# Gate and value projection units moved between attention's steps and the linear attention's levels, two barriers taken out, attention scores two deep

## What is computed

```
def trunk_layer(x, cond, lp, lam_init, cache):
    sh1, sc1, g1, sh2, sc2, g2, sh3, sc3, g3 = jnp.split(cond.astype(x.dtype), N_MOD, -1)
    ...
    h = x * (1.0 + sc2) + sh2
    m, new_cache = token_mixer(h, lp, lam_init, cache)
    x = layer_norm(ALPHA * x + g2 * m, lp['ln_g'][1], lp['ln_b'][1])
    ...

def token_mixer(h, lp, lam_init, cache):
    p = h @ lp['w_in']
    p_rw, p_gla, p_diff = jnp.split(p, [RW_IN, RW_IN + GLA_IN], -1)
    ...
    o_rw, s_rw = rwkv7_branch(p_rw, s_rw0, lp)
    o_gla, s_gla = gla_branch(p_gla, s_gla0, lp)
    o_diff, new_k, new_v = diff_branch(p_diff, ctx_kv, lp, lam_init)
    mixed = jnp.concatenate([o_rw, o_gla, o_diff.astype(F32)], -1)
    out = mixed @ lp['w_out']
```

## Time and profile before

| what | value |
|---|---|
| median of 3 runs | 2019.07 us (2018.96 to 2021.9) |
| the profiled execution's own time | 2014.65 us |
| its span (first to last instruction) | 2012.7 us |
| PE, DVE, ACT busy | 95%, 51%, 36% of the span |
| chain of work that ended last | PE 83%, DVE 9%, ACT 4%, waiting for nothing shown 2% |

### The profile page before, as it was taken

The page is one execution under the profiler, slowest core; times in us unless marked ns, Lnnn a source line. Parts: engine busy times, 40 slices in busy tenths (PEclk is TensorE's granted clock), DMA queues, the critical chain, the costliest instruction groups (busy, mean ns, idle before and its releaser), DMA issues.

```text
span 2012.7 us, 37360 instructions
## 1 busy us (share of the span) xinstructions
PE 1913.7 (95%) x16184; PEld 1724.1 (86%) x16184; DVE 1019.8 (51%) x1639; ACT 726.2 (36%) x1210; POOL 32.5 (2%) x66
## 2 busy tenths in 40 slices
PE   7999999998899899999999999999988789999997
PEld 5999997987679769999989999989867787899996
DVE  2333334555566775333355333366557757633335
ACT  3322224444442353222252222255364325422222
POOL 0000000000000001000000000000000000000000
PEclk9999999999989999999999999999999899999999
DMA  8733336333581145333344333323345003433330
GB/s 343 303 125 125 124 123 234 105 119 132 227 334 43 36 158 190 125 124 124 124 156 146 125 124 125 125 84 126 108 159 209 4 4 137 159 124 124 123 109 32
DMA packets 41472, 277.70 MB, mean 138 GB/s; under 512 B 4778, under 2 KB 6810, under 8 KB 9344
## 3 DMA queue, kind: packets, MB, share of 16 engines
q1 hardware_dynamic: 35424, 255.34, 35.1%
q0 software_dynamic: 3312, 16.91, 2.2%
q10 hardware_dynamic: 2608, 3.56, 0.5%
HBM read 269.22 MB, written 3.41 MB: 135 GB/s over the span
## 4 chain that ended last, share of the span: by engine, by line
PE 83%; DVE 9%; ACT 4%; issue 2%; DMA 1%; ACTq 0%; PEldq 0%; DVEq 0%; SPq 0%; PEld 0%
PE bank L923 17%; PE bank L992 17%; PE bank L927 17%; PE bank L926 17%; PE bank L760 2%; PE bank L1380 1%; PE bank L1369 1%; DMA ring<-weights 1%; PE bank L1387 1%; DVE ring_r L2193 1%; PE bank L841 1%; ACT arena L1663 1%; PE bank L769 1%; DVE arena L2203 1%; DVE arena L2229 1%
## 5 line engine op out<-in xcount | busy, mean ns | idle before, releaser
L2193 DVE TENSOR_TENSOR ring_r<-ring,arena_r 128x1024 fp32r<-128x1024 f32 x328 | 387.9, 1222 | 679.3 <-ACT arena_r L1658 678.6
L923 PE MATMUL bank<-arena_r 128*128 128x384 f32 (+3 forms) x2052 | 702.2, 342 | 8.9 <-DVE arena_r L2237 6.7
L927 PE MATMUL bank<-arena_r,ring_r 128*128 128x384 f32 (+2 forms) x1812 | 602.0, 332 | 0.0
L926 PE MATMUL bank<-arena_r 128*128 128x384 f32 (+2 forms) x1812 | 599.7, 331 | 0.0
L923 PEld LDWEIGHTS bank<-arena_r 128*128 128x128 f32 x2052 | 386.5, 188 | 31.6 <-issue 15.7
L1658 ACT ACTIVATE arena_r<-ring 128x1024 fp32r<-128x1024 f32 x340 | 340.7, 1052 | 144.4 <-PE bank L927 138.9
L926 PEld LDWEIGHTS bank<-arena_r 128*128 128x128 f32 x1812 | 340.9, 188 | 3.4
L927 PEld LDWEIGHTS bank<-arena_r,ring_r 128*128 128x128 f32 x1812 | 340.1, 188 | 0.0
L992 PE MATMUL bank<-arena_r 128*128 128x512 f32 x1128 | 310.6, 393 | 0.3 <-issue 0.3
L1812 ACT ACTIVATE arena<-bank 128x384 f32<-128x384 f32 x88 | 43.2, 491 | 738.4 <-PE bank L927 738.4
L992 PEld LDWEIGHTS bank<-arena_r 128*128 128x128 f32 x1128 | 210.8, 188 | 43.1 <-issue 1.2
(11 more groups left out here) (301 smaller groups left out, 1809.6 us busy)
## 6 DMA issues: line engine op xcount, KB each, us to landing
ring<-weights SPq DMA_DIRECT2D x242, 1024.0 KB, 4.9
lnrow<-ln_in POOLq DMA_DIRECT2D x6, 1024.0 KB, 6.5
const<-consts POOLq DMA_DIRECT2D x1, 2211.0 KB, 10.0
arena<-gate POOLq DMA_DIRECT2D x4, 385.0 KB, 7.5
x<-x_in ACTq DMA_DIRECT2D x1, 1536.0 KB, 13.7
rows<-row_in POOLq DMA_DIRECT2D x2, 704.0 KB, 10.4
par<-par_in POOLq DMA_DIRECT2D x2, 662.5 KB, 7.5
y_out<-x SPq DMA_DIRECT2D x2, 512.0 KB, 2.6
```

Of the source, the lines that this page charges most:

```text
L923: mm = pe.matmul(out, w_h, h_h, start=start, stop=False, skip_group_check=True)
L926: pe.matmul(out, w_h, h_l, start=False, stop=False, skip_group_check=True)
L927: return pe.matmul(out, w_l, h_h, start=False, stop=stop, skip_group_check=True)
L2193: ve.tensor_tensor(low_unit((l, name), u) if out is None else out, raw, place.bitcast(F32), ALU.subtract).then_inc(w_ready, 1)
```

## The change

It moves the GLA gate and value units out of `project`. The gates' 12 blocks (4 units x 3 groups, `gate_block`) stand in attention's steps, three in step 0 and one in each of steps 1 to 9; the values' three blocks (`value_block`) stand at the beginning of `gla` and before levels 1 and 2. Their rounding moves with them: units 6 to 9 in steps 1, 4, 7 and 10 on ACT and 2, 5, 8 and 11 on DVE. The gates are copied out of PSUM in ACT's step 10, and Silu is applied later, after the last level, from SBUF. The two barriers before `attention` and before `gla` go. Scores have two pairs of banks in place of three, the turned weights take bank 7, and the result of values(i - 3) goes into the last 128 columns of the bank that scores(i) fills; PE does values(i - 3) before scores(i). The rotary products stand after units 0 to 3. In the stream `gate1` goes behind `next0` (layer 0) or behind `shift2` (layer 1); its selecting and copying moves from `attention` to `rwkv`. The first half of `shift2` rides at the end of `attention`, the other half in the second direction's levels. Dummy products: 4, 4 and 6 where there were 7, 7, 7 and 10 in `gla`, and 14 new ones in layer 1's `rwkv`. POOL moves the rates when the value blocks are done. ACT's square root for GLA moves to the end of `rwkv`.

```diff
-        parts += [("feat", N_FEAT), ("tokm", N_TOKM), ("gate1", 4), ("shift2", 8)]
+        parts += [("feat", N_FEAT), ("tokm", N_TOKM - 1), ("shift2", 4), ("last_tokm", 1), ("rest2", 4)]
         if l + 1 < DEPTH:
-            parts += [("next0", 8), ("next1", 8)]
+            parts += [("next0", 8), ("gate1", 4), ("next1", 8)]
+        else:
+            parts += [("gate1", 4)]
...
-SCORE_BANK = (2, 4, 0)
+SCORE_BANK = (0, 5)
+GATES_TOKM = 4
+VALUES_TOKM = 8
+GATE_BLOCKS = (3, 4, 5, 6, 7, 8, 9, 10, 11, 12)
+VALUE_BANK = (5, 6, 5)
...
-WARM_START, WARM_MIX, WARM_TURN, WARM_GLA = 6, 6, (10, 6, 10), (7, 10)
+WARM_START, WARM_MIX, WARM_TURN, WARM_GLA, WARM_UNITS = 6, 6, (10, 6, 10), (4, 6), 14
...
-ROPE_AT = (1, 2, 4, 5)
+ROPE_AT = (0, 1, 2, 3)
...
+                    def gate_block(b):
+                        m, g = GATES_TOKM + b // GROUPS, b % GROUPS
+                        if b == 0:
+                            pe.wait_ge(feat_out, 2 * N_FEAT + 1)
+                            pe.wait_ge(rates_ready, 8)
+                        if g == 0:
+                            pe.wait_ge(w_ready, UNITS[l, "tokm"] + m + 1)
+                        mm = wide_part(m, g, ps[2 + g])
...
+                    def value_block(g):
+                        pe.wait_ge(w_ready, UNITS[l, "tokm"] + 2 * N_TOKM)
...
                     def attention():
-                        ada, t = FIRST[l, "gate1"], NMIX * l + 1
+                        ada, n = FIRST[l, "shift2"], SHIFT_RIDE[NMIX * l + 2]
+                        pe.wait_ge(rope_done, 4)
+                        pe.wait_ge(tokm_out, GROUPS)
...
                         for i in range(GROUPS * HEADS + 3):
+                            if i >= 3:
+                                values(i - 3)
                             if i < GROUPS * HEADS:
                                 scores(i)
                             if 2 <= i < GROUPS * HEADS + 2:
                                 turn(i - 2)
-                            if i >= 3:
-                                values(i - 3)
-                            if i == GROUPS * HEADS - 1:
-                                pe.wait_ge(exp_done, GROUPS * HEADS - 2)
-                                ride_product(pe, ada, SCORE_BANK[0])
...
+                            if i < len(GATE_BLOCKS):
+                                for b in range(GATE_BLOCKS[i - 1] if i else 0, GATE_BLOCKS[i]):
+                                    gate_block(b)
+                            elif i == 10:
+                                pe.wait_ge(tokm_out, 2 * GROUPS)
+                                ride_product(pe, ada, 2)
+                            elif i == 11:
+                                ride_product(pe, ada + 2, 3)
+                            elif i < 14:
+                                ride_turn(pe, n + i - 12, 4, 8 * (i - 12))
...
                         def outputs(u):
                             ve.wait_ge(att_mm, u + 1)
+                            if u + 3 < GROUPS * HEADS:
+                                ve.wait_ge(scores_mm, u + 4)
...
                     turn_x(1)
                     project()
-                    meet()
                     attention()
-                    meet()
                     gla()
```

More of the change, by code:

```diff
@@ L1122, in project, with wide_part @@
                                           start=True, stop=True).then_inc(rope_mm, 1)
-                        pe.drain().then_inc(used, 1)
+                    def wide_part(m, g, bank):
+                        hi, lo = proj_w_hi[:, m % HI_PROJ, :], low_unit((l, "tokm"), m)
+                        t = slice(g * P, g * P + P)
+                        for i in range(2):
+                            k, c = 2 * (m % GATES_TOKM) + i, slice(i * 512, i * 512 + 512)
+                            mm = three(bank[:, :], (h_hi[:, k, t], mix_h_lo[:, k, t]), (hi[:, c], lo[:, c]),
+                                       k == 0, k == KT - 1, used if m % 2 == 0 and i == 0 and g == 0 else None)
+                        return mm
@@ new lines, in value_block @@
+                    def value_block(g):
+                        pe.wait_ge(w_ready, UNITS[l, "tokm"] + 2 * N_TOKM)
+                        if g == 2:
+                            pe.wait_ge(tokm_out, 2 * GROUPS + 1)
+                        t = slice(g * P, g * P + P)
+                        for k in range(KT):
+                            m, c = VALUES_TOKM + k // 4, slice(k % 4 * 256, k % 4 * 256 + 256)
+                            hi, lo = proj_w_hi[:, m % HI_PROJ, :], low_unit((l, "tokm"), m)
+                            mm = three(ps[VALUE_BANK[g]][:, 0:256], (h_hi[:, k, t], mix_h_lo[:, k, t]), (hi[:, c], lo[:, c]),
+                                       k == 0, k == KT - 1)
+                        mm.then_inc(tokm_mm, 1)
+                        if g == GROUPS - 1:
+                            pe.drain().then_inc(used, 1)
@@ L1317, in rwkv @@
                         mm.then_inc(values_mm, 1)
+                        t, wide_ada = NMIX * l + 1, FIRST[l, "gate1"]
                         if not last:
@@ L2007, in gla @@
-                        ride_copy(sc, n + 3, 0)
-                        if not last:
-                            ride_copy(sc, n + 4, 1)
-                            ride_copy(sc, n + 5, 3)
+                            if u <= GROUPS:
+                                tokm_read(2, u - 1)
+                        ride_copy(sc, n + 3, 5)
+                        ride_out(sc, n + 3, 7, 2, 8, 2)
+                        sc.wait_ge(tokm_out, 2 * GROUPS)
+                        for d in range(2):
+                            sc.activation(gd[:, d, :, :], gd[:, d, :, :], ACT.Silu).then_inc(tokm_out, 1)
@@ L2011, in gla @@
+                        sc.activation(table_col, eps_col, ACT.Exp)
+                        ride_copy(sc, n + 4, 1)
+                        ride_copy(sc, n + 5, 3)
                         for d in range(2):
@@ L2476, in project @@
                                 lam_end()
-                        for m in range(2 * N_TOKM):
+                        for m in range(GATES_TOKM + HI_PROJ):
                             rest_unit("tokm", m, proj_w_hi[:, m % HI_PROJ, :])
```

390 lines of the change are left out of this document (215 added, 175 removed).

## The result

The changed kernel takes 2044.53 us (median of 4 runs, 2040.17 to 2045.05) against 2019.01 before: a ratio of 1.011, 95% interval 1.0083 to 1.0138, so **slower by 25.5 us** (the interval stands for 17 to 28 us). The side was forecast, the size was not: 2027, with a range up to 2040. The profiled execution took 2044.24 us with a span of 2042.4, 29.7 more than before's.

A forecast was written before the change was run, and what follows sets the result against it. Attention and levels were taken as bound by a PE-DVE-ACT chain, `project` by PE. Terms -0.6 + 0.2 - 2.5 + 2.9 + 8.9 - 2.0 + 1 = +7.9 gave median 2027 us; own range 2023 to 2036, for all 2005 to 2040.

The forecast's parts named there:

- The loop: Attention's steps: scores, maxima, exponentials, copy of turned weights and values form a closed loop, 4.84 us a step.
- C: Whole kernel comes out even, the removed barrier's wait returning for the last rotation: 2015 to 2023, named 2019; chance 0.17.
- D: Faster, PE's idle in attention and levels takes the moved work in: 2008 (1998 to 2015); chance 0.28.
- Step 10: Attention's step 10: the riding product waits for the gates' copies in ACT's list, about 9.0 us before scores(11).
- The clock: Granted clock falls behind an idle of some 2 us at attention's new start: +1 in both layers together.
- its range for all: Whole kernel's time: 2005 to 2040, leaving out the better half of D and most of B.
- Levels: Linear attention, level 0's end to the turned keys: 33.2 us in each layer, -2.5 in layer 0, +2.9 in layer 1.
- Layer 0's `rwkv`: Transposes to the units' first products: two added products, two selects and a gate copy's wait, +8.9 us.
- its upper bound: Layer 0's rwkv: 13 us added if the four more chunks of 1 MB arrive late.
- stages that the forecast put at 0: Includes the stretches from units' first products to layer 1's A and from layer 1's recurrence to PE's end: 0.
- Rival B: Clock falls to 1.2 GHz in attention's steps, loop 6.5 us, +20: 2047 (2036 to 2056); chance 0.10.

The follow-up runs named there:

- clock_only: Changed kernel with dummy products alone: eight before the last rotation's wait, fourteen in step 10, fourteen for six before layer 1's turned keys; 2032.09 us.
- dummies: Changed kernel with fourteen dummy products in place of six ahead of layer 1's turned keys; 2036.27 us.
- three_parts: Changed kernel with turned-weights copy and step 10's gate copies ahead of ACT's exponentials, and fourteen dummies before layer 1's turned keys; 2012.05 us.
- copy_first: Changed kernel with ACT's copy of the turned weights of unit i - 2 ahead of the exponentials of unit i; 2021.19 us.
- five_parts: three_parts plus eight dummies ahead of the last rotation's wait, and gate copies also ahead of step 10's copy of the turned weights; 2005.98 us.
- five_light: five_parts with only 128 columns loaded of each of layer 0's four gate1 chunks; 2007.39 us.

## Why the forecast was wrong in size

- **The loop: right.** 4.84 us a step was forecast (its pieces sum to 4.86), 4.94 measured, and the edit that breaks it gives 3.39, near the sum of PE's work of 3.5. Rivals C and D fall with it: the idle of the earlier trace rows grew.
- **Step 10: right but for the clock.** 9.0 was forecast, 10.95 and 10.83 measured, 9.03 with the clock kept up.
- **The clock: the step that failed.** The forecast priced it at "+1 in both layers together", for the new start alone. By its own pieces (3.2 us round the loop to PE, 1.9 for square and gate copies, less 0.36 for the transposes) PE idles some 4.7 us in step 10, ahead of the riding product; 4.57 were measured. Yet it took that product at full clock (1.93, with the gap behind it 2.22), where 3.64 was due. And it let layer 1's way from the turned keys to the transposes cost 0, since "DVE sets the pace, and the change puts nothing on it"; with fewer dummies, 2.05 us of idle stand in front, and 5.7 us came of it. By the stages the term is 11.0: 1.6 at the start of layer 0, 1.9 and 1.8 in step 10, 5.7 behind the turned keys; by the median of `clock_only` it is 12.4. With that in its place the forecast's sum, 7.9 - 1 + 12.4 = 19.3, gives 2038 on the median. That is within its range for all, up to 2040, though above the forecast's own, up to 2036.
- **Levels: right in size**, -1.3 and +4.1 for -2.5 and +2.9.
- **Layer 0's `rwkv`: +10.2 for +8.9, in part by luck.** The forecast saw PE go "without a break" there in the kernel before, and did not see that a part ran at half clock:

```profile
583.92 6.24 PE L760 MATMUL bank<-ring,silu_c 128*32 128x256 f32 x64
```

The same products take 4.00 in the changed kernel (584.64). That kernel waits 2.67 us for chunks (0.66, 0.24, 0.54 and 1.23), which the forecast had in its upper bound alone. In the variants with all loads the stretch took from 33.3 to 37.0 us.
- **What remains** is about 6 us by the medians; the interval, which begins at 17 us, does not tell it from nothing. In the profile it lies in stages that the forecast put at 0. Of the +4.6 in the last stretch, a piece of 10 us at half clock in the second feed-forward (see below) makes 4.3, and other executions need not have it. Of the +3.9 between layer 0's units and layer 1's start, 2.7 arise by the first products behind the barrier at the end of the units; that way took 90.8 us before and 91.9 to 93.8 in the changed kernel and all its variants. A part of it is the moved square root, which the forecast put at nothing in layer 0: on ACT it now stands last ahead of the barrier in front of the units (its table load takes 1.28 us at 615.69), and PE waits there for ACT. Before, then now:

```profile
604.56 1.98 PE L1287 MATMUL bank<-arena 64*64 64x128 f32 x32 [0.39 <-DVEq L712]
617.29 1.99 PE L1339 MATMUL bank<-arena 64*64 64x128 f32 x32 [2.18 <-ACTq L727]
```

This is read from the rows; no run moved the square root back, and the rest of the +3.9 stays open.
- **Rival B** named the clock, but in the wrong place. The long steps kept 1.00 with 1.27 us of idle in each 4.94. The Trainium skill, "TensorE: Matmul & The Clock Gate", section "A second HAM failure mode: psum-queue depth-cycling", tells of a kernel in which frequent small idles made the clock go up and down; the trace of these steps does not show that at this size. The clock fell behind single idles of 2.05 to 4.57 us, though not behind each: behind the same 2.11 us, scores(0) to scores(1) took 6.35 in layer 0 and 4.78 in layer 1, and in `dummies` 4.79 and 6.31. And the half clock at 583.92 above (0.61 granted from 583.90 to 590.20) stands behind no such idle: in the 20 us ahead of it PE's idles are 0.47 us at most.

## What to carry to other kernels

When a result goes into a buffer that a later step fills, follow the ring of waits through every in-order queue, and look in it for an instruction that stands behind one it does not need: here a copy behind the next step's exponentials made 1.5 us a step. Price each idle of PE that a new order opens twice, once as the wait and once as the half-speed work that may follow it, and count the dummy products that were removed. Try the queue's order in the old kernel too, so that its gain is not counted for the move. A gain of one edit moves the bottleneck to the next queue, as the gate copies showed, so look at the combination's own profile.

## What the runs showed of the hardware that was not expected

With PE busy throughout, the granted clock sometimes falls to half for about 10 us: the changed kernel at 1753.30 to 1763.40, shown above, costing 4.3 us against the same rows before. The windows of `three_parts`' profiled execution, which took 2023.15 us where its median is 2012.05, hold two such pieces:

```profile
759.00:768.80 9.80, 9.80 (x42) 9.80 (x42) 4.21 (x6) 3.38 (x6) 3.19 (x5) 0.51 0.28 100
1059.50:1069.40 9.90, 9.90 (x42) 9.90 (x42) 3.88 (x6) 3.38 (x6) 0.00 (x0) 0.50 0.25 83
```

The profiles of `copy_first`, `five_parts` and `five_light` hold one each (from 1739.0, 1714.3 and 756.0). All six begin 2.4 to 2.8 us behind the same place in a feed-forward, where PE takes up products of 128 columns after an idle of 0.72 us (1750.90 in the changed kernel). That place comes three times in an execution, 39 times in the thirteen profiles, and the other 33 times full clock was kept behind the same idle. So the idle does not decide it alone, and what does was not settled. The ten executions of `copy_first` go from 2013.74 us at a mean granted clock of 0.983 to 2029.68 at 0.974, so falls of the clock are a part of the scatter; how much of it such pieces make is not shown, since one execution of each kernel left rows.
